# Norms, adds and squares of a two-model stack cut into halves of 512 columns

## The reference, cut to what matters

```python
def rmsnorm(x, g):
    xf = x.astype(jnp.float32)
    y = xf * lax.rsqrt(jnp.mean(xf * xf, axis=-1, keepdims=True) + NORM_EPS)
    return y.astype(x.dtype) * g

    # first model, each of two layers: mixer, attention over mem, squared-relu MLP
    x = x + rmsnorm(y, g[1])
    h = rmsnorm(x, g[2])
    x = x + rmsnorm(memory_cross_attention(h, mem_n, ...), g[3])
    h = rmsnorm(x, g[4])
    x = x + rmsnorm(squared_relu_mlp(h, w_ff1[l], w_ff2[l]), g[5])

    # second model, each of two layers
    h = h + 0.5 * swiglu(rms_norm(h, ffn1_norm[layer]), ...)
    h = h + attention(rms_norm(h, mix_norm[layer])) @ w_o
    h = h + 0.5 * swiglu(rms_norm(h, ffn2_norm[layer]), ...)
    ...
    return rms_norm(h, final_norm)
```

## Time and profile before

| | us |
|---|---|
| median of 3 runs | 1823.01 |
| lowest and highest | 1821.73, 1823.05 |
| span of the profiled execution | 1820.1 |
| TensorE busy in it | 1786.4 |
| VectorE, ScalarE, GpSimd busy | 1153.3, 860.8, 73.9 |

### The profile page before, as it was taken

The page is one execution under the profiler, slowest core; times in us unless marked ns, Lnnn a source line. Parts: engine busy times, 40 slices in busy tenths (PEclk is TensorE's granted clock), DMA queues, the critical chain, the costliest instruction groups (busy, mean ns, idle before and its releaser), DMA issues.

```text
span 1820.1 us, 25737 instructions
## 1 busy us (share of the span) xinstructions
PE 1786.4 (98%) x10450; PEld 1543.6 (85%) x10450; DVE 1153.3 (63%) x1150; ACT 860.8 (47%) x1042; POOL 73.9 (4%) x118
## 2 busy tenths in 40 slices
PE   9999999999999999999999999999999999999998
PEld 7989888888988878888888898888888888788886
DVE  7665466557566465556666654666676666876665
ACT  7545455545555455545343455433353334553343
POOL 1000000000220000000000011000000000110000
PEclk9999999999999999999999999999999999999999
DMA  9426355556546355555555534555555555336552
GB/s 319 170 74 227 107 195 185 184 186 201 174 167 204 120 171 186 184 186 173 192 178 188 185 119 147 178 194 184 184 184 185 189 185 185 116 119 206 186 183 93
DMA packets 217156, 318.07 MB, mean 175 GB/s; under 512 B 5585, under 2 KB 179809, under 8 KB 217074
## 3 DMA queue, kind: packets, MB, share of 16 engines
q1 hardware_dynamic: 212274, 300.96, 49.2%
q0 software_dynamic: 4800, 15.94, 2.8%
HBM read 315.83 MB, written 1.05 MB: 174 GB/s over the span
## 4 chain that ended last, share of the span: by engine, by line
PE 93%; DVE 4%; ACT 2%; issue 0%; DMA 0%; SPq 0%; ACTq 0%; DVEq 0%
PE Y L1802 29%; PE C L1728 23%; PE C L1729 11%; PE Y L1758 9%; PE C L1758 5%; PE C L1770 4%; PE Y L1696 3%; DVE xn L1168 1%; DVE w_lo L1127 1%; ACT xn L672 1%; PE C L2001 1%; PE C L2130 1%; PE C L1974 1%; PE Y L2021 1%; PE C L2290 1%; PE C L2013 1%
## 5 line engine op out<-in xcount | busy, mean ns | idle before, releaser
L1127 DVE TENSOR_TENSOR w_lo<-raw,w_hi 128x2048 fp32r<-128x2048 f32 x282 | 645.8, 2291 | 323.5 <-ACT w_hi L657 323.0
L657 ACT ACTIVATE w_hi<-raw 128x2048 fp32r<-128x2048 f32 x282 | 538.3, 1910 | 251.0 <-PE Y L1802 165.0
L1728 PE MATMUL C<-at_hl,w_hi 128*128 128x512 f32 x1440 | 511.3, 398 | 0.0
L1729 PE MATMUL C<-at_hl,w_lo 128*128 128x256 f32 x1440 | 404.2, 281 | 0.0
L1728 PEld LDWEIGHTS C<-at_hl,w_hi 128*128 128x128 f32 x1440 | 270.6, 188 | 66.2
L1729 PEld LDWEIGHTS C<-at_hl,w_lo 128*128 128x128 f32 x1440 | 271.9, 189 | 2.1
L1802 PE MATMUL Y<-w_hi,hid_h 128*128 128x512 f32 x696 | 217.2, 393 | 0.0
L1802 PE MATMUL Y<-w_lo,hid_h 128*128 128x512 f32 x696 | 215.5, 391 | 0.0
L1802 PE MATMUL Y<-w_hi,hid_l 128*128 128x512 f32 x696 | 214.5, 389 | 0.0
L1802 PEld LDWEIGHTS Y<-w_lo,hid_h 128*128 128x128 f32 x696 | 130.6, 188 | 28.9
L1802 PEld LDWEIGHTS Y<-w_hi,hid_l 128*128 128x128 f32 x696 | 130.6, 188 | 28.5
(11 more groups left out here) (292 smaller groups left out, 2268.5 us busy)
## 6 DMA issues: line engine op xcount, KB each, us to landing
raw<-in_ffn_w_in SPq DMA_DIRECT2D x88, 1024.0 KB, 5.0
raw<-in_w_ff SPq DMA_DIRECT2D x64, 1024.0 KB, 5.6
raw<-in_ffn_w_out SPq DMA_DIRECT2D x44, 1024.0 KB, 4.8
raw<-in_w_mem_kv SPq DMA_DIRECT2D x16, 1024.0 KB, 5.7
raw<-in_w_qkv SPq DMA_DIRECT2D x12, 1024.0 KB, 5.4
raw<-in_sb_w_qkv SPq DMA_DIRECT2D x12, 1024.0 KB, 5.1
raw<-in_w_in_ab SPq DMA_DIRECT2D x8, 1024.0 KB, 9.1
raw<-in_w_mem_q SPq DMA_DIRECT2D x8, 1024.0 KB, 5.2
```

The source lines that it names most:

```text
L657: nc.scalar.activation(w_hi[:, n % RING, :], raw[:, n % RAW, :], ACT.Copy).then_inc(hi_split, 1)
L1127: V.tensor_tensor(w_lo[:, n % RING, :], raw[:, n % RAW, :], w_hi[:, n % RING, :].bitcast(f32), ALU.subtract).then_inc(lo_split, 1)
L1728: mm(tiles(to, 2), wh[:, k, part], hl[:, k, :, :], start=k == 0, stop=False)
L1729: last = mm(to[:, S:2 * S], wl[:, k, part], hl[:, k, 0, :], start=False, stop=k == KT - 1)
```

## The change

- Every norm scale, post add and add runs on two halves of 512 columns, and each half signals for itself: `x_ready` and `xn_ready` now count four a norm or add. `turn_block` waits for its half of xn ahead of each four transposes. The output leaves in four DMAs of 256 KB.
- `row_chunk` does the last chunk of a layer sorted by column half, all 6 products of half 0, then the 6 of half 1, and a new semaphore `y_half` goes up at the end of each half (the very last still is `chunk_done`).
- The square and the estimate are cut in two as well (`halves_guess`), but for the first norm and that of mem, which keep the whole form. The first half's sum goes through two small Identity instructions to become the bias of the second half's Ln and Identity, and ScalarE waits for the second of them (`again`) before it squares the second half.
- In `post_ahead` VectorE's `lo` is cut in two (`lo_part`): its first half stays in its place, its second goes behind `norm_lo` of block 0.

```diff
+            def halves_guess(srcs, done, b, at):
+
+                j = 2 * at.rms + b
+                act.wait_ge(*done[0])
+                square(srcs[0], xn[:, b, HALF[0]], stat[:, 0, j:j + 1])
+                nc.scalar.activation(stat[:, 5, j:j + 1], stat[:, 0, j:j + 1], ACT.Identity, bias=eps[:, 1:2], scale=4.0 / D)
+                again(nc.scalar.activation(stat[:, 7, j:j + 1], stat[:, 0, j:j + 1], ACT.Identity, bias=eps[:, 2:3], scale=-4.0 / D))
+                act.wait_ge(*done[1])
+                square(srcs[1], xn[:, b, HALF[1]], stat[:, 8, j:j + 1])
+                guess(stat[:, 8, j:j + 1], (stat[:, 5, j:j + 1], stat[:, 7, j:j + 1]), j)
...
+            def square(src, to, total):
+
+                squares[0] += 1
+                nc.scalar.activation(to, src, ACT.Square, accum_out=total).then_inc(squared, 1)
+                act.wait_ge(squared, squares[0])
...
+            def post_block(b, at, shift=0):
+
+                rms(b, at, shift)
+                for h in range(2):
+                    scaled(Y[:, 2 * b + h, :], b, h, at).then_inc(dve_seq, 1)
+                for h in range(2):
+                    dve.wait_ge(dve_seq, seq[0] + h + 1)
+                    V.tensor_tensor(x[:, b, HALF[h]], x[:, b, HALF[h]], xn[:, b, HALF[h]], ALU.add).then_inc(x_ready, 1)
+                seq[0] += 2
...
             def post_ahead(at, then):
 
-                post_scale(0, at)
-                post_add(0)
-                lo(then.chunk - 1 + AHEAD)
+                post_block(0, at)
+                lo_part(then.chunk - 1 + AHEAD, 0)
                 norm_scale("at", then, [0], -1)
-                post_scale(1, at, 1)
-                post_add(1)
+                post_block(1, at, 1)
                 norm_lo("at", then, C, [0])
+                lo_part(then.chunk - 1 + AHEAD, 1).then_inc(lo_split, 1)
                 norm_scale("at", then, [1])
                 norm_lo("at", then, C, [1])
...
             def add(factor, at, blocks=range(TB)):
                 for b in blocks:
-                    if b == 0:
-                        dve.wait_ge(y_ready, at.y)
-                    else:
-                        dve.wait_ge(chunk_done, at.chunk)
-                    V.scalar_tensor_tensor(x[:, b, :], Y[:, 2 * b:2 * b + 2, :].rearrange(flat), factor, x[:, b, :],
-                                           ALU.mult, ALU.add).then_inc(x_ready, 1)
+                    for h in range(2):
+                        dve.wait_ge(*y_done(b, h, at))
+                        V.scalar_tensor_tensor(x[:, b, HALF[h]], Y[:, 2 * b + h, :], factor, x[:, b, HALF[h]],
+                                               ALU.mult, ALU.add).then_inc(x_ready, 1)
...
+                    part = slice(b * P, (b + 1) * P)
+                    order = [(k, j, half) for k in parts for j in range(3) for half in range(2)]
+                    for k, j, half in sorted(order, key=lambda o: o[2]) if end else order:
+                        still, moving = ((h[k], wh), (h[k], wl), (l[k], wh))[j]
+                        closes = end and k == 1 and j == 2
+                        last = mm(Y[:, 2 * b + half, :], still[:, part], moving[:, k, half * 512:(half + 1) * 512],
+                                  start=first and k == 0 and j == 0, stop=closes)
+                        if closes and (b, half) != (1, 1):
+                            last.then_inc(y_half, 1)
...
                 for h in range(2):
+                    pe.wait_ge(xn_ready, before_norm + 2 * b + h + 1)
                     for k in range(4):
                         last = nc.tensor.transpose(banks[:, 2 * b + h, k * P:(k + 1) * P],
```

More of the change, by code:

```diff
@@ L225, in build @@
         up_used = sem("up_used")
-        y_ready = sem("y_ready")
+        y_half = sem("y_half")
         squared = sem("squared")
@@ L389, in counts @@
             if s[0] == "norm":
-                return dict(norm=1, rms=s[1] != "same", xn=2, turned=4 * (s[1] != "out"))
+                return dict(norm=1, rms=s[1] != "same", xn=2 * TB, turned=4 * (s[1] != "out"))
             if s[0] == "post":
-                return dict(norm=1, rms=1, x=2)
+                return dict(norm=1, rms=1, x=2 * TB)
             if s[0] == "meanwhile":
-                return dict(norm=2, rms=2, x=2, xn=2, turned=4, chunk=len(s[1]), copied=len(s[1]))
+                return dict(norm=2, rms=2, x=2 * TB, xn=2 * TB, turned=4, chunk=len(s[1]), copied=len(s[1]))
             if s[0] == "add":
-                return dict(x=2)
+                return dict(x=2 * TB)
             if s[0] == "cols":
@@ L399, in counts @@
             if s[0] == "even_cols":
-                return dict(norm=1, rms=1, xn=2, turned=4, chunk=len(s[1]), copied=len(s[1]))
+                return dict(norm=1, rms=1, xn=2 * TB, turned=4, chunk=len(s[1]), copied=len(s[1]))
             if s[0] == "rows":
@@ L667, in hi_back, with guess, whole_guess @@
                 nc.scalar.activation(w_hi[:, n, 1024:2048], raw[:, n, 1024:2048], ACT.Copy).then_inc(hi_split, 1)
[L669 to L675, removed]
+            squares = [0]
+            def square(src, to, total):
+                squares[0] += 1
+                nc.scalar.activation(to, src, ACT.Square, accum_out=total).then_inc(squared, 1)
+                act.wait_ge(squared, squares[0])
+            def guess(total, at_eps, j):
+                ln = nc.scalar.activation(stat[:, 1, j:j + 1], total, ACT.Ln, bias=at_eps[0], scale=4.0 / D)
+                nc.scalar.activation(stat[:, 3, j:j + 1], total, ACT.Identity, bias=at_eps[1], scale=-4.0 / D)
                 again(ln)
                 nc.scalar.activation(stat[:, 2, j:j + 1], stat[:, 1, j:j + 1], ACT.Exp, scale=-0.5).then_inc(guessed, 1)
+            def whole_guess(src, b, at):
+                j = 2 * at.rms + b
+                square(src, xn[:, b, :], stat[:, 0, j:j + 1])
+                guess(stat[:, 0, j:j + 1], (eps[:, 1:2], eps[:, 2:3]), j)
+            def halves_guess(srcs, done, b, at):
+                j = 2 * at.rms + b
+                act.wait_ge(*done[0])
[5 more added lines that the diff above has]
+                guess(stat[:, 8, j:j + 1], (stat[:, 5, j:j + 1], stat[:, 7, j:j + 1]), j)
             def norm_guess(to, at, behind_rows=False):
@@ L697, in norm_hi, with x_guess, y_guess @@
                                              tiles(banks[:, 2 * b + h, :], 4), ACT.Copy).then_inc(at_hi, 1)
[L699 to L704, removed]
-                if b == 0:
-                    act.wait_ge(y_ready, at.y)
-                else:
-                    act.wait_ge(chunk_done, at.chunk)
-                guess(Y[:, 2 * b:2 * b + 2, :], b, at, shift)
+            def x_guess(b, at):
+                halves_guess([x[:, b, HALF[h]] for h in range(2)], [(x_ready, at.x - 2 * TB + 2 * b + h + 1) for h in range(2)], b, at)
+            def y_guess(b, at):
+                halves_guess([Y[:, 2 * b + h, :] for h in range(2)], [y_done(b, h, at) for h in range(2)], b, at)
             def add_ahead(then):
@@ L1128, in lo, with lo_part @@
                                 ALU.subtract).then_inc(lo_split, 1)
+            def lo_part(n, k):
+                dve.wait_ge(hi_split, n + 1)
+                part = (slice(None), n % RING, slice(k * 1024, (k + 1) * 1024))
+                return V.tensor_tensor(w_lo[part], raw[:, n % RAW, k * 1024:(k + 1) * 1024], w_hi[part].bitcast(f32), ALU.subtract)
             def lo_front(n):
```

66 lines of the change are left out of this document (28 added, 38 removed).

## The result

The changed kernel takes **1832.7 us** (median of 4 runs, 1830.8 to 1833.7) against 1823.0 for the kernel before: ratio 1.0051, 95% interval 1.0038 to 1.0065. In a second measurement, beside other runs of before, it took 1830.0 (1829.0 to 1831.0), ratio 1.0041, 1.0028 to 1.0055. So it is slower by 8 to 10 us. The forecast was 1829.4, range 1824.5 to 1834.

The account below looks back on a forecast made before the run. TensorE, busy 1786.4 of 1820.1 us, was taken as the bound, its lengthened waits paid in full. Boundary terms summed to +6.6 (+6.4 unrounded), span 1826.5, plus 2.9 to the median: 1829.4 us, range 1824.5 to 1834.

Parts of the forecast that it names:

- The price of a guess in halves: On ScalarE, each square and estimate in halves takes 0.83 us more than whole (bounds 0.52 and 0.95).
- the clock: Rival: longer TensorE pauses make its granted clock fall, one to three times; 1831 to 1836 us, chance 0.20.
- relu_ff(0): Ahead of relu_ff(0), two longer x guesses delay `norm_lo`, for which TensorE waits: +1.7 us.
- the banded attention: Ahead of the banded attention, `norm_lo` and TensorE's start move later behind two longer guesses: +1.7 us.
- second `post_ahead`: At the second `post_ahead`, `norm_lo` of block 0 comes later behind post 1: +0.5 us.
- the swiglus: At two `add_ahead` ahead of a swiglu, longer x guess 1 and half scales delay `lo`: +1.0 us each.
- tail: After the last product, half adds, squares and a smaller last DMA end sooner: -1.1 us (-0.8 to -1.4).
- first `post_ahead`: At the first `post_ahead`, longer guesses make the transposes of block 1 start later: +1.3 us.
- The start: At the kernel's start, xn's first half is 0.5 us early but ScalarE's first `hi` holds `norm_hi` back: 0.
- Attention and kv: At two `add_ahead` there, block 0 wins 0.80 us but block 1's third pass waits: +0.2 us each.
- The offset: For the whole kernel, the median time lies 2.9 us above the profiled span.
- halves hand over sooner: Rival: xn's early first half decides TensorE's start at boundaries, and the tail shortens; about 1818.8 us, chance 0.05.

Follow-up runs that it names:

- run 1: Changed kernel with the guess on x made whole again, the rest left in halves; 1820.9 us, ratio 0.9990.
- run 2: Kernel before, nothing halved, with ScalarE copying 752 columns ahead of each guess at the two boundaries of two mem chunks; 1827.5 us, ratio 1.0028.
- runs 1, 5 and 6: Changed kernel: 1, x guess whole; 5, also 8 dummy products in first swiglu; 6, every guess whole except last norm's, 6 dummies; 1820.9, 1819.6, 1819.0 us.
- run 8: Changed kernel with x guess whole, dummies in the first swiglu, and the scale to xn whole in all norms but first and last; 1820.5 us, ratio 0.9989.
- run 7: Changed kernel with x guess whole, dummies in the first swiglu, and the last chunk's products in the order of before; 1824.6 us, ratio 1.0011.
- again: The changed kernel itself, unaltered, measured and profiled a second time; 1830.0 us (1829.0 to 1831.0).
- run 3: Kernel before with only the guesses on x and Y made in two halves, all else whole; 1842.8 us, ratio 1.0112.
- run 10: Changed kernel with the guess on x whole only at the two boundaries of two mem chunks, relu_ff(0) and banded attention; 1826.2 us, ratio 1.0020.

## Why the prediction was right or wrong

**The price of a guess in halves** was right to 0.01 us (0.83), and it is the cause: undoing it on x alone (run 1) turns the change from slower to faster, and a copy as long as the extra, with nothing halved (run 2), makes the same boundaries late.

**The boundaries, with the clock up**, came out as worked out: with dummies in the pauses relu_ff(0) +1.69 and the banded attention +1.75 (1.7 and 1.7), second `post_ahead` +0.54 (0.5), the swiglus +0.99 and +1.00 (1.0 each), tail -1.16 (-1.1). The first `post_ahead` was +1.10 (1.3). The start varies by a microsecond either way from one profile to the next; the -0.5 there is no effect of the change. In the waits ahead of the swiglu, w_lo is the releaser, with 1.08 us where the earlier trace rows have 0.34 (forecast 1.3):

```profile
1171.71 1.21 PE L1723 MATMUL Y<-w_lo,at_hl 128*128 128x256 f32 x8 [1.08 <-DVE w_lo L1151]
```

**Attention and kv** were too dear by 0.2 to 0.8: xn of block 0 does come while TensorE still multiplies (no wait, 0.80 in the earlier trace rows), and the wait for block 1 grows from 1.66 to 1.98, as said; but the stick stretch ended at 0.0 instead of +0.2, and kv with `double` at +0.5 including a fall of the clock, -0.45 with dummies and without the fall. All terms together were too dear: +4.8 us between the profiles with the clock up, against the sum's +6.6.

```profile
1041.63 1.35 PE L1884 MATMUL C<-ident,xn 128*128 128x128 f32 x8 [1.98 <-DVE xn L1194]
1357.80 1.76 PE L1884 MATMUL C<-ident,xn 128*128 128x128 f32 x8 [1.98 <-DVE xn L1194]
```

**The step that failed** is the clock. The prediction had it as a rival of 0.20 with 1831 to 1836, not as a term of the sum, though its own sum made pauses of 2.1 to 2.9 us at five places and the earlier trace rows show the clock falling about 2 us into one. The measured 1830.0 and 1832.7 are the forecast mechanism and this rival together. That they lie so near 1829.4 is in part luck: the sum was too high by 1.8 us (0.4 of it is the start) and the offset by 1.1, and the clock that it left out made up for both and more. In the spans it is worth 6.6 us in the first profile (11.4 against 4.8 with dummies) and 4.3 in the second; in the medians 3 to 6. A few tenths of this may be the dummies' and not the clock's: the stick attention, where the clock never fell, also has -0.23 with them against +0.01 and -0.10. The argument used against the clock, that no pause of before did it, named the one of 1.26 us; the longest there behind the start are two of 1.66, and they say nothing of longer ones:

```profile
1032.19 1.09 PE L1856 MATMUL C<-ident,xn 128*128 128x128 f32 x8 [1.66 <-DVE xn L1168]
```

Nor is the 2 us of the earlier trace rows a fixed delay. Behind the last product, where TensorE has nothing more to do, the clock fell 2.1 us later in the profile of before, but 4.8 and 4.6 us later in the two of the changed kernel (last products at 1824.8 and 1822.5):

```profile
1829.00:1829.50 0.50, 0.00 (x0) 0.00 (x0) 0.08 (x1) 0.00 (x0) 0.00 (x0) 1.00 0.41 156
1829.50:1830.00 0.50, 0.00 (x0) 0.00 (x0) 0.00 (x0) 0.00 (x0) 0.00 (x0) 0.56 1.05 389
```

```profile
1827.00:1827.50 0.50, 0.00 (x0) 0.00 (x0) 0.00 (x0) 0.00 (x0) 0.00 (x0) 0.61 1.01 377
```

The Trainium skill, page "TensorE: Matmul & The Clock Gate", section "What's actually happening", has idling bring the lower clock back; these traces agree that it comes back, and show it behind waits of 1.6 to 2.5 us.

**The offset.** I added 2.9 us to the span to come to the median. In all runs the time is 1.8 us above the span; the other 1.1 was that the profiled run of before, 1820.1, was a short one (its runs' spans go from 1819.5 to 1821.8). So of 11.4 and 9.1 us between the profiles only 9.7 and 8.1 stand in the medians, and with dummies +4.1 of 4.8.

**The rival "halves hand over sooner"** gave 1818.8 if a guess in halves cost under 0.3 us. With the guess whole, so that it costs nothing, runs 1, 5 and 6 came to 1820.9, 1819.6 and 1819.0. The rule of the Trainium skill, page "Perfetto Trace Analysis", section "Optimizing Scalar/DVE Operations", thus holds for this kernel's scales to xn (run 8) and not for the squares: broken up, these wait for themselves. The reordered products (run 7) cut no instruction. Not shown by itself is how much the self-wait and how much the second read and Identity cost; the timeline gives the whole, 1.26 us from square to square.

## What to carry to other kernels

Split an operation that hands its result on (here the scale), order the last products so that one half is complete early, and leave whole an operation whose parts must be joined again on its own engine: here 0.83 us a time on an engine busy for 48%. Put the clock into the sum wherever a change lengthens TensorE's waits to those behind which it fell here, 1.6 to 2.5 us: a fall cost 0.9 to 1.6 us, and 2.6 where it lasted twice as long. Eight or nine dummy products in the pause took it away here, and cost nothing, as they ended before what was waited for.

## What the runs showed of the hardware

I had not expected that **the same pause in the same kernel lowers the clock in one run and not in another, or at one place and never at another**. All stretches of the lower clock between the start and the tail lasted 3.4 or 6.8 us.

| wait ahead | profiles | clock fell |
|---|---|---|
| relu_ff(0), 1.88 to 1.93, then 0.68 to 0.69 | changed, again, run 3, run 2 | 6.8 us, 3.4 us, 3.4 us, no |
| banded attention, 2.23, 2.22, 1.91, 1.91, 1.91 | changed, again, run 2, run 3, run 7 | yes, no, yes, no, no |
| first swiglu, 1.93 to 1.94 | changed, again, runs 1 and 10 | in all four |
| kv, 1.98 | changed, again, run 10 | in all three |
| stick attention, 1.97 to 1.98 | changed, again, run 10 | in none |
| block 1 of stick attention and kv, 1.66 | before, run 2 | in none |
| block 1 of stick attention and kv, 1.72 and 1.73 | run 8 | in none |
| block 0 of stick attention and kv, 1.64, then 0.34 | run 3 | at kv |
| the two `post_ahead` and block 1 of stick attention, 2.42, 2.06, 2.50 | run 3 | at all three |
| `double`, 1.67 | run 3 | no |

The rows around the stick and the kv wait are alike (waits of 0.34, then 1.98), yet the clock never fell at the one and always at the other. What decides between them is open: no run here varied the pause or its place by itself.
